# Attention of the first mixer in pairs of heads: 64-row and 64-column halves of TensorE's array

## The reference

```python
h = rms_norm(x, attn_norm_g)
proj = h @ w_in                      # 1024 -> 5128
qa, ka, va, qb, kb, vb, f_logit, g_logit = split(proj)
# "block" attention, 8 heads of 64. With 256 tokens there is one block, so it is causal attention
qa, ka = rope(rms_norm(qa)), rope(rms_norm(ka))
o_a = softmax(causal(qa @ ka.T / 8)) @ va
# "forgetting" attention, 8 heads of 64, c = cumsum(log_sigmoid(f_logit + b_forget))
qb, kb = rms_norm(qb), rms_norm(kb)
o_b = softmax(causal(qb @ kb.T / 8 + c[t] - c[s])) @ vb
gates = sigmoid(g_logit + b_gate)    # 2 x 1024 columns
x = x + (gates[0] * (o_a @ w_branch_moba) + gates[1] * (o_b @ w_branch_fox)) @ w_out
```

## Time and profile before

| | us |
|---|---|
| median of 3 runs (868.4 to 872.04) | 869.7 |
| the profiled execution | 871.05 |
| its span, first to last instruction | 868.8 |
| TensorE busy, share of the span | 92% |
| VectorE, ScalarE, POOL busy | 63%, 56%, 10% |
| granted TensorE clock, mean | 0.969 |

### The profile page before, as it was taken

One profiled execution on the slowest core, in us unless ns is written; L12 is line 12 of the kernel. 1 busy time (PEld: TensorE's weight loads), 2 busy tenths in 40 slices (PEclk: granted clock), 3 DMA queues, 4 the chain that ended last, 5 costly groups with the idle time before them and its releaser, 6 DMA issues.

```text
span 868.8 us, 10702 instructions
## 1 busy us (share of the span) xinstructions
PE 797.1 (92%) x3811; PEld 647.7 (75%) x3811; DVE 550.6 (63%) x817; ACT 485.9 (56%) x743; POOL 86.6 (10%) x50
## 2 busy tenths in 40 slices
PE   4989999999799999999999798796859999999998
PEld 3777788777588888888887577663637888888886
DVE  5676676567556777776463477687673666665650
ACT  4755656666236777774264744342543677776630
POOL 0023000000000000000000056644231000000000
PEclk9989999999999999999999899798969999999999
DMA  8766333344237655456383533221001675554550
GB/s 303 292 203 198 103 116 119 97 147 140 68 120 251 211 193 193 151 170 204 105 270 124 179 98 97 78 68 49 25 25 48 215 237 182 177 184 173 191 165 24
DMA packets 70566, 130.21 MB, mean 150 GB/s; under 512 B 5534, under 2 KB 17142, under 8 KB 70142
## 3 DMA queue, kind: packets, MB, share of 16 engines
q1 hardware_dynamic: 69662, 124.90, 44.2%
q10 hardware_dynamic: 864, 4.78, 1.5%
HBM read 128.61 MB, written 1.05 MB: 149 GB/s over the span
## 4 chain that ended last, share of the span: by engine, by line
PE 74%; DVE 11%; ACT 7%; DMA 4%; issue 2%; POOL 1%; SPq 1%; ACTq 0%; DVEq 0%; POOLq 0%
PE acc L478 20%; PE acc L480 20%; PE acc L479 20%; DMA b_raw<-in_w_in 2%; DVE b_wlo L1186 2%; PE banks L579 2%; PE banks L704 2%; PE banks L539 2%; PE banks L564 2%; PE banks L717 1%; DMA b_raw<-in_w_mem_kv 1%; ACT b_whi L825 1%; PE banks L552 1%; PE banks L543 1%; PE banks L566 1%
## 5 line engine op out<-in xcount | busy, mean ns | idle before, releaser
L1186 DVE TENSOR_TENSOR b_wlo<-b_raw,b_whi 128x1024 fp32r<-128x1024 f32 (+4 forms) x222 | 253.1, 1179 | 102.8 <-ACT b_whi L825 101.4
L825 ACT ACTIVATE b_whi<-b_raw 128x1024 fp32r<-128x1024 f32 (+4 forms) x244 | 234.3, 1001 | 77.1 <-DMA b_raw<-in_w_in 19.3
L478 PE MATMUL acc<-b_whi,b_hhi 128*128 128x512 f32 (+4 forms) x528 | 205.0, 388 | 10.3 <-DVE b_hlo L1459 4.6
L479 PE MATMUL acc<-b_whi,b_hlo 128*128 128x512 f32 (+4 forms) x528 | 198.2, 375 | 0.0
L480 PE MATMUL acc<-b_wlo,b_hhi 128*128 128x512 f32 (+4 forms) x528 | 197.8, 375 | 0.0
L478 PEld LDWEIGHTS acc<-b_whi,b_hhi 128*128 128x128 f32 x528 | 100.9, 191 | 31.0 <-DVE b_hlo L1459 5.1
L480 PEld LDWEIGHTS acc<-b_wlo,b_hhi 128*128 128x128 f32 x528 | 100.8, 191 | 15.8
L479 PEld LDWEIGHTS acc<-b_whi,b_hlo 128*128 128x128 f32 x528 | 100.8, 191 | 15.8 <-issue 1.5
L478 PE MATMUL acc<-b_whi,b_ohi 128*128 128x512 f32 (+1 forms) x272 | 105.8, 389 | 5.4 <-DVE b_wlo L1186 2.9
L480 PE MATMUL acc<-b_wlo,b_ohi 128*128 128x512 f32 (+1 forms) x272 | 103.4, 380 | 0.0
L479 PE MATMUL acc<-b_whi,b_olo 128*128 128x512 f32 (+1 forms) x272 | 103.1, 379 | 0.0
(11 more groups left out here) (214 smaller groups left out, 909.0 us busy)
## 6 DMA issues: line engine op xcount, KB each, us to landing
b_raw<-in_w_in SPq DMA_DIRECT2D x48, 512.0 KB, 4.8
b_raw<-in_w_ffn_up SPq DMA_DIRECT2D x40, 512.0 KB, 4.8
b_raw<-in_w_ffn_in SPq DMA_DIRECT2D x40, 512.0 KB, 4.7
b_raw<-in_w_ffn_down SPq DMA_DIRECT2D x22, 512.0 KB, 6.0
b_raw<-in_w_ffn_out SPq DMA_DIRECT2D x22, 512.0 KB, 4.7
b_raw<-in_w_out SPq DMA_DIRECT2D x16, 512.0 KB, 3.7
b_raw<-in_w_in SPq DMA_DIRECT2D x12, 412.0 KB, 3.6
b_raw<-in_w_in SPq DMA_DIRECT2D x8, 410.0 KB, 3.5
```

What stands on the lines that cost most here:

```text
L478: nc.tensor.matmul(o, a, wh, start=first, stop=False)
L479: nc.tensor.matmul(o, b, wh, start=False, stop=False)
L825: A(whi[:, n % SPLIT, 0:c["nk"], 0:c["n"]], raw[:, n % RAW, 0:c["nk"], 0:c["n"]], ACT.Copy)\
L1186: V.tensor_tensor(wlo[:, n % SPLIT, 0:c["nk"], 0:c["n"]], raw[:, n % RAW, 0:c["nk"], 0:c["n"]], whi[:, n % SPLIT, 0:c["nk"], 0:c["n"]].bit ...
```

## The change

Heads work in pairs g (heads 2g and 2g+1). The scores of a pair are issued alternately for rows 0 to 63 into bank 0 and rows 64 to 127 into bank 1; the decay product gets 64 rows in each half too, with zeros in unused rows (`pick` is now 128 x 8 x 128 and loaded ahead of "kb"; `c8` has 128 rows, cleared by POOL, and is filled at rows 0 and 64). The transposes of a pair go to banks 2 and 3, and each is copied by its own ScalarE instruction. The value products of both heads go to bank 2, columns 0 to 63 and 64 to 127, and leave it in one high and one low instruction. Maxima are negated, and sums inverted, once for a pair. Pairs alternate between two buffers for the probabilities (`Sm` and `xn`).

The order of `MIX1` is new: a slot holds one pair and two parts of projections, the divide stands in the slot of its own scores, and the value products follow the same pair's transposes after one part. The group "vb" moves behind "fg0".

```diff
-        FILL = [[("qb", 1)], [("kb", 0)], [("kb", 1)], [("vb", 0)], [("vb", 1)], [("fg0", 0), ("fg0", 1)],
-                *[[(f"fg{n}", c)] for n in range(1, 5) for c in range(2)],
-                [("bra0", 0)], [("bra1", 0)], [("brb0", 0)], [("brb1", 0)]]
-        BEHIND = {0: [("sums", "qb")], 2: [("turn", "qb"), ("sums", "kb")], 4: [("turn", "kb"), ("sums", "vb")],
-                  5: [("sums", "fg0")], 6: [("decay sums", 0)],
-                  **{5 + 2 * n: [("mix", n - 1), ("sums", f"fg{n}")] for n in range(1, 5)},
-                  14: [("mix", 4), ("sums", "bra0")], 15: [("sums", "bra1")]}
-        for s, fill in enumerate(FILL):
-            MIX1 += [("scores", s)] if s < 16 else []
-            MIX1 += [("divide", s - 1)] if 1 <= s < 17 else []
-            MIX1 += BEHIND.get(s - 1, [])
-            MIX1 += [("gemm", *part) for part in fill]
-            MIX1 += [("probs", s - 1)] if 1 <= s < 17 else []
-            MIX1 += [("pv", s - 2)] if s >= 2 else []
+        SLOTS = [([("qb", 1)], [("kb", 0)]), ([("kb", 1)], [("fg0", 0)]), ([("fg0", 1)], [("vb", 0)]),
+                 ([("vb", 1)], [("fg1", 0)]), ([("fg1", 1)], [("fg2", 0)]), ([("fg2", 1)], [("fg3", 0)]),
+                 ([("fg3", 1)], [("fg4", 0)]), ([("fg4", 1)], [("bra0", 0)]), ([("bra1", 0), ("brb0", 0)], [("brb1", 0)])]
+        BEFORE = {3: [("decay sums", 0)], 8: [("sums", "bra0")]}
+        BEHIND = {0: [("sums", "qb")], 1: [("turn", "qb"), ("sums", "kb")], 2: [("sums", "fg0"), ("turn", "kb")],
+                  3: [("sums", "vb")], **{3 + n: [("mix", n - 1), ("sums", f"fg{n}")] for n in range(1, 5)},
+                  8: [("mix", 4), ("sums", "bra1")]}
+        for s, (one, two) in enumerate(SLOTS):
+            MIX1 += [("scores", s)] if s < 8 else []
+            MIX1 += BEFORE.get(s, [])
+            MIX1 += [("gemm", *part) for part in one]
+            MIX1 += [("divide", s)] if s < 8 else []
+            MIX1 += BEHIND[s]
+            MIX1 += [("probs", s - 1)] if s else []
+            MIX1 += [("gemm", *part) for part in two]
+            MIX1 += [("pv", s - 1)] if s else []
...
+            def pair_scores(g):
...
+                rows = (slice(0, 64), slice(64, P))
+                for t, c0, c1 in ((1, 0, S), (0, S, S + P)):
+                    mm = [nc.tensor.matmul(X[i][:, c0:c1], qT[n][r, b, t * P:(t + 1) * P], kT[n][r, b, 0:c1 - c0],
+                                           start=True, stop=not n) for i, r in enumerate(rows)]
+                    if n:
+
+                        mm = [nc.tensor.matmul(X[i][:, c0:c1], pick[r, 2 * b + i, :], c8[r, 0:c1 - c0],
+                                               start=False, stop=True) for i, r in enumerate(rows)]
...
+            def pair_T(g):
+
+                pe.wait_ge(*at("probs ready", f"{g}"))
+                for i in range(2):
+                    claim(2 + i, f"probs {g}")
+                    for c, to in enumerate((1, 2, 0)):
+                        mm = nc.tensor.transpose(X[2 + i][:, to * P:(to + 1) * P],
+                                                 pair_probs(g, i)[:, c * P:(c + 1) * P], ident)
+                    full(mm, 2 + i, f"probs {g}")
+
+            def pair_pv(g):
+
+                for i in range(2):
+                    pe.wait_ge(*at(f"bank{2 + i} free", f"probs {g}"))
...
+                claim(2, f"pv {g}")
...
+                for i in range(2):
+                    nc.tensor.matmul(o[i][:, 0:S], v[i][:, 0, :], PT[i][:, 0:S], start=True, stop=False)
+                for i in range(2):
+                    mm = nc.tensor.matmul(o[i][:, P:S], v[i][:, 1, :], PT[i][:, S:S + P], start=False, stop=True)
+                full(mm, 2, f"pv {g}")
...
+            def pair_out(g):
+
+                if g:
+                    act.wait_ge(*at("bank2 full", f"pv {g - 1}"))
+                for i in range(2):
+                    act.wait_ge(*at(f"bank{2 + i} full", f"probs {g}"))
+                    done(A(PT[i][:, 0:384], X[2 + i][:, 0:384], ACT.Copy), f"bank{2 + i} free", f"probs {g}")
...
-                    done(A(c8[:, :], X[0][0:8, 0:S], ACT.Copy, scale=-1.0), "bank0 free", "decay sums")
+                    act.wait_ge(sem("decay rows cleared"), 1)
+                    A(c8[0:8, :], X[0][0:8, 0:S], ACT.Copy, scale=-1.0)
+                    done(A(c8[64:72, :], X[0][0:8, 0:S], ACT.Copy, scale=-1.0), "bank0 free", "decay sums")
...
+            def pair_max(g):
+
+                if g >= 2:
+                    dve.wait_ge(*at("bank3 full", f"probs {g - 2}"))
+                for i in range(2):
+                    dve.wait_ge(*at(f"bank{i} full", f"scores {g}"))
...
+                    done(ins, f"bank{i} free", f"scores {g}")
+                for i in range(2):
+                    dve.wait_ge(*at(f"bank{i} free", f"scores {g}"))
...
+            G.memset(c8[:, :], 0.0).then_inc(sem("decay rows cleared"), 1)
```

More of the change, by code:

```diff
@@ L90, in constants @@
         c[:, C_CS + 16 * i + 8:C_CS + 16 * i + 16] = np.sin(angle[i * P:(i + 1) * P])
-    return c, g, np.ascontiguousarray(np.eye(8, dtype=np.float32)[:, :, None].repeat(P, 2))
+    pick = np.zeros((P, 8, P), np.float32)
+    for h in range(8):
+        pick[h, h], pick[64 + h, h] = 1, 1
+    return c, g, pick
 def plan():
@@ L253, in program @@
         lt = sb("lt", [P, 2, T, 8])
-        c8 = sb("c8", [8, S])
+        c8 = sb("c8", [P, S])
         rp = sb("rp", [P, 4, T, 8, 8])
@@ L523, in tok_T @@
                     full(mm, bank, step)
+            def pair_scores(g):
+                n, b = g // 4, g % 4
+                for i in range(2):
+                    claim(i, f"scores {g}")
+                if b == 0:
+                    for step in ("qb", "kb") if n else ("qa", "ka"):
+                        pe.wait_ge(*at(f"bank{T_BANKS[step][-1]} free", f"{step}T"))
+                if g == 4:
+                    pe.wait_ge(*at("bank0 free", "decay sums"))
+                    pe.wait_ge(sem("pick in"), 16)
+                rows = (slice(0, 64), slice(64, P))
[6 more added lines that the diff above has]
+                for i in range(2):
+                    full(mm[i], i, f"scores {g}")
@@ L525, in attn_scores @@
             def attn_scores(j):
-                q, k, _, _, whole = head(j)
+                q, k, _, whole = head(j)
                 b = j % 2
                 claim(b, f"scores {j}")
-                for start, steps in ((0, ("qa", "ka")), (8, ("qb", "kb")), (16, ("sqk",)), (20, ("mq", "mk"))):
+                for start, steps in ((16, ("sqk",)), (20, ("mq", "mk"))):
                     if j == start:
@@ L550, in attn_T @@
                 pe.wait_ge(*at("probs ready", f"{j}"))
-                for c, to in enumerate((1, 3, 0, 2) if head(j)[4] else (1, 2, 0)):
+                for c, to in enumerate((1, 3, 0, 2) if head(j)[3] else (1, 2, 0)):
                     mm = nc.tensor.transpose(X[2][:, to * P:(to + 1) * P], probs(j)[:, c * P:(c + 1) * P], ident)
@@ L555, in attn_pv @@
             def attn_pv(j):
-                _, _, v, _, whole = head(j)
+                _, _, v, whole = head(j)
                 pe.wait_ge(*at("bank2 free", f"probs {j}"))
-                for start, step in ((0, "va"), (8, "vb"), (16, "sviq"), (20, "mkv")):
+                for start, step in ((16, "sviq"), (20, "mkv")):
                     if j == start:
@@ L794, in _ @@
                         small(hgain[:, head, :], name, "small in")
+                if n == groups["kb"]["first"]:
                     sp.dma_start(pick[:, :, :], dram["pick"]).then_inc(sem("pick in"), 16)
```

114 lines of the change are left out of this document (71 added, 43 removed).

## The result

The changed kernel takes 880.23 us, the median of 5 runs (877.47 to 881.54), against 869.7 of the kernel before (5 runs beside it, 866.37 to 872.77): a ratio of 1.011, 95% interval 1.0088 to 1.0132. It is slower, by 1.1%. The forecast was 879, with a range of 865 to 889. The profiled execution took 880.66 us with a span of 878.9.

A forecast was written before the change was run, and what follows sets the result against it. TensorE bounded the old kernel; paired, hand-overs between VectorE and ScalarE were to make it wait. Walk +4.4, clock +2.4 and +3 give +9.8 us on 869.7 (median) or 871.05 (profiled): 879, own range 874 to 886, overall 865 to 889.

The forecast's parts named there:

- The 21.6 us: TensorE work saved by pairing: 1.8 us for each of four block pairs, 3.6 for each of four forgetting pairs.
- The loop of slots 4 to 7: Gate-work slots: VectorE and ScalarE hand over for 15.8 us per slot, 17.2 with 512-column chunks; TensorE idles 3 to 4.
- the walk: Slot-by-slot sum of hand-overs through the attention stretch, without clock: first stage 65.2 us, second 79.2, together +4.4.
- Slots 0 to 3: First stage, from first scores at 79.38: slots end at 91.5, 106.4, 130.4 and 144.6 us, with 10.4 us idle in slot 2.
- the named releaser: ScalarE's kT copy, said to end TensorE's idle of about 10 us before the transposes of pair 1 in slot 2.
- The clock: Pauses lower TensorE's clock: 2.4 us after slot 2's idle, 3 after the four shorter pauses (half of 6).
- Rival 1: TensorE stays the bound because the copies run early enough: 849 us, chance 0.09.
- Rival 2: Slot 2: fg0 work does not in effect precede the kb copies, while the slots' loop holds: 864 us, chance 0.08.
- Rival 3: The clock stays up and one long wait is shorter by a few us: 866 to 874, taken as 871, chance 0.13.
- Rival 4: Pairs do not overlap: scores +0.64 or +1.3 us and value products +0.8 per pair; 888 us, chance 0.10.
- point of decision: Slots 4 to 7: a pair exceeding its forecast by 0.4 us makes TensorE's path pass the engines' loop.
- Edits costed at nothing: Larger pick table (0, bound 2 us) and POOL's c8 clearing (0); vb's move and fewer low parts counted in the walk.

The follow-up runs named there:

- e7: e6's order, but each pair's second head waits for the first in scores and value products; 865.91 us, ratio 0.9931 to the kernel before.
- e6: Changed kernel with entries reordered in all slots (divide a slot later, kb's turn and copies ahead of gate work); 851.57 us, ratio 0.9769 to before.
- e4: Changed kernel, same order, but the second head's scores in each pair wait until the first's are complete; 885.02 us, ratio 1.0161 to before.
- e3: Changed kernel plus 76 filler matmuls of 512 columns in TensorE's pauses, results thrown away; 872.79 us, ratio 1.0011 to before.
- e1: Changed kernel with one entry moved: in slot 2 the turned kb is copied before the fg0 gate work; 871.12 us, ratio 1.0006 to before.

## Why the prediction was right, step by step

**The bound before, and what TensorE saves: right.** The block pair (0.92 to the last end), the forgetting pair (1.51 against 1.5) and the value products (0.80 against 0.79) came as costed. The value taken for the column halves had no row behind it and might have been 1.58; the lower end was the true one, and e7 shows what it saves. One term was sized too high: the transposes of a pair take 0.57 us at the full clock (144.94 to 145.52, then the projection starts), not 0.73. The pair sums were rounded up on both sides: the forecast's own terms make 3.0 instead of 3.2 us for a forgetting pair and 6.6 instead of 6.8 for the two heads before, which leaves the difference as it was. The 21.6 us are real: in e6, with a single low-clock stretch of 3.4 us, TensorE is busy for 54.16 + 62.18 = 116.3 us of the stretch, 20.7 less than the 137.0 of the earlier trace rows.

**Program order.** The two halves' products start 0.01 us apart, and a pair takes the 1.51 us that e4's second head takes alone. The Trainium skill (TensorE: Matmul & The Clock Gate, Part 3, "What overlaps and what doesn't") says that matmuls start and end strictly in program order. The kernel before speaks against it: all four 256-column products of index heads 0 and 1 start ahead of head 0's 128-column ones at 533.39 us, though head 1's stand behind those in the program. The pairs don't test the rule, since their halves are issued alternately, and it asks for no delay between them.

**The loop of slots 4 to 7: right, to the step.** Forecast 12.9 us from max to value products, measured 12.97; forecast loop 15.8, and the pair maxima of the four gate slots are 16.6, 15.8 and 18.1 apart. The middle one is the bare loop; the forecast for the third was 17.2 for its wide chunks. With the clock up (e3) the distances are 15.9, 15.8 and 17.0, so the lower clock makes 0.7 us of the first and 1.1 of the third. The terms of the walk hold one by one as well: max to exps 1.57 us (forecast 1.43), exps 1.77 (1.8), splits 2.77 (2.77), divide 1.13 (1.11), gate work 4.78 (4.79), first copy to value products 0.95 (1.03). The idles were said to be 3 to 4 us and are 3.29, 2.73, 4.21 and 2.23.

**Slots 0 to 3: right.** TensorE was to end slots 0 to 3 after 12.1, 14.9, 24.0 and 14.2 us, with 2.4 us of clock in slot 2, so 26.4. Measured: 12.0, 15.2, 26.4, 14.2. The idle before the transposes of pair 1 was to be 10.4 and is 10.26, from the named releaser, and e1 shows that the fg0 work ahead of it makes 7.2 of it. The 0.9 us before the decay sums are there too (0.93).

**The clock: right in sum.** 2.4 and 3 were taken, the second as half of its bound of 6; e3 measures 2.4 and 3.0. The granted clock was 0.5 from 119.0 to 132.7 us, 13.7 us long, which is longer than the 6.9 that the earlier trace rows made me expect, but about 8 of it were the pause itself, in which it cost nothing. It fell behind three of the four shorter pauses: for 3.4, 6.8 and 3.4 us. The walk without any clock said 65.2 and 79.2; with the fillers the stages are 65.3 and 78.7. The 3 was a guess between bounds: nothing in the rows told which of the four pauses would bring the lower clock.

**The total.** Forecast +9.8 on the stretch, measured +9.4; the medians differ by 10.5, the profiled executions by 9.6. The start of the stretch is 3.9 us later by scatter, and 3.1 us come back after it (the stretch ends 13.2 us later than before, the span 10.1 later); in the second block's mixer the low-clock stretches add up to 37.5 us, against 44.3 in the kernel before, which fits. So the exactness of the median has luck in it. That of the stretch rests on the walk, which holds term by term, and on luck only where half of a bound was taken for the clock's 3 us.

**The rivals.** Rival 1 (TensorE stays the bound, 849) did not come, but not for want of room: e6 is that case at 851.6, and what stood against it was the order of entries. Rival 2's picture (no fg0 work ahead of the kT copy, 864) is e1's edit; there 3.07 us of idle remain, and e1 takes 871. Its 864 took away too much: it had the whole idle go, while the copy still waits for the pair's exps and splits, and it left out the clock, which still costs about 3 us of stage 2 in e1 (81.6, against 78.7 in e3). Rival 3's 871 has its case in e3, in which the clock stays up: 872.8. Rival 4 (no overlap, 888) was worked out for scores and value products together; e4, with the scores alone, gives 885, and both together were tried only in e6's order (e7). Its point of decision, 0.4 us above my figures, can't be read from one kernel, and was not tried.

**Edits costed at nothing.** The larger pick table cost TensorE nothing: it is issued at 64.41 us, and from 68.06 us to the first scores TensorE waits only 0.83 us, for the copy of kT, as in the kernel before. In the stretch no wait of TensorE names a load, and ScalarE waits 2.2 us for a weight load, once.

## What to carry to other kernels

When a change takes work off the engine that is the bound, walk the chain of hand-overs that its next input comes through, in the order in which each engine takes its entries: two engines at 55% can hold a third at a loop a third too long. Put what others wait for (copies out of a bank, a turned operand) ahead of what nobody waits for in this slot, per engine, before judging the change itself. A pause of the matrix engine costs a second time where its clock falls afterwards (12.5 us of pauses before value products cost 3.0 more). And what a saving is worth depends on the order around it: of the time that overlap saves on TensorE, a little over half reached the stretch in one order, over four fifths in the other.

## What the runs showed of the hardware

- The two column halves overlap completely although both write the same bank: 0.80 us for two heads, against 0.79 for one before, and 1.72 when the second waits for the first. No row of the kernel before had shown it.
- Products that are issued alternately for two row or column halves start 0.01 us apart.
- Scores that alternate between 64 rows and 8 cost 2.08 us a head, for every one of the eight forgetting heads; with 64 rows in both, 1.51 (e4's second head). The larger operand, mostly zeros, is the cheaper one.
- The length of a pause did not tell whether the lower clock follows: behind pauses of 3.29, 4.21 and 2.23 us it did, for 3.4, 6.8 and 3.4 us; behind 2.73 us it did not; behind 3.07 (e1) it lasted 6.8 us and behind 3.08 (e6) 3.4.
- Doing 17.5 us of useless matmuls in pauses made the kernel 7.4 us faster: the granted clock stayed at 1.00 (2.4 GHz) over the whole stretch, where it averaged 0.90 and 0.92 and was at 0.5 (1.2 GHz) for 27 us without them.
